# Attention turns with unnormalised probabilities, the reciprocals spread by TensorE onto the outputs, and part c's products made in the input projection

## The chip, the cores and the metric

One core of a Trainium2 chip runs the whole program. The metric is the device time of one execution in microseconds (us), the median of several.

## What is computed

One step of a two-layer streaming encoder over 576 tokens: 512 of a new stream and 64 of a running one. Each layer makes one combined input projection and, from it, three parts: A, sliding-window attention; B, a gated MLP over positions; C, retention. The three are scaled, joined and projected by `w_out`; then a SwiGLU feed-forward follows. Each half ends in a norm and is added to the stream. The change is in A, and in the place of C's last product:

```
s = einsum('...lhgd,...mhd->...hglm', q, k) * HEAD_DIM**-0.5      # own chunk of 64 and two chunks before
p = softmax(concatenate([s, sink], -1))[..., :-1]                 # a learned sink per head joins the sum
a = einsum('...hglm,...mhd->...lhgd', p, v)
...
c = head_group_norm(r, ret_g) * silu(g_c)
merged = concatenate([rms_norm(a), rms_norm(b), c]) @ w_out
```

## The kernel before

Everything is kept transposed, features on partitions and tokens along the free axis. The tokens are cut into two groups, 256 (g = 0) and 320 (g = 1), for the large products. Each of these is made in float32 precision of three passes (L454 to L456): a weight tile is split into a high half (ScalarE, `w_hi`) and a low half (VectorE, `w_lo`, L1230), and so is the moving side (`h_hi`, `h_lo`). The order of each engine's work is written out by hand; semaphores tie the engines. ScalarE's work is recorded at one line, L878, whatever it is.

Attention runs after the input projection, in nine chunks of 64 queries, eight heads in four pairs. It is a pipeline by turns. In turn c

- TensorE makes the scores of chunk c+1 (L707, 64x64 tiles, banks 0/1 or 2/3), the transposes of the probabilities of chunk c-1 (`turn`: L722, the first 128 keys; L724, the other 64), and the values of chunk c-2 (`values`, L744: a wide part of 128 keys, a half part of 64);
- VectorE takes the maxima of chunk c (L1484 to L1488), copies the half transposes of chunk c-2 to `halfT` (L1496), adds the sink to the sum of chunk c-1 and inverts it (L1503, L1504), and multiplies the probabilities by it (`normalise`, L1505). Then come one product of the merged input of `w_out` (`merged`, L1518) and one low half of such a product (`lo_of_merged`, L1524);
- ScalarE makes the exponentials of chunk c with their sums, copies the wide transposes to `wideT`, after every second chunk takes the output of a pair of chunks from PSUM (a copy `aT` and a square `sqa`, by `outs`), and makes the high half of one product (`hi_of_merged`).

The merged input has 8 tiles of 128 rows for each group: k = 0 to 3 are A, 4 and 5 are B, 6 and 7 are C. The table `MERGED` (L151) gives their order. The first 8 (B and C) are made in the turns, the 8 of A after the last turn. Outputs of a pair of chunks go to bank 6 or 7 in turn. The last values come between the first output products (`part_out`, tiles of B and C first). GpSimd adds up the squares of A.

In the list below are the functions that the change touches.

## Time and profile before

| | |
|---|---|
| Median of 3 runs | 1372.68 us (1370.81 to 1374.32) |
| The profiled execution | 1367.82 us, of it 1365.8 us of span |
| Busy: TensorE, VectorE, ScalarE, GpSimd | 97%, 49%, 35%, 13% |
| Instructions in the record | 24010 |
| Granted clock of TensorE over the span | 0.992 |

Busy time counts the share of the span in which an engine had an instruction under way. It says nothing of which engine the others waited for; for that one reads the stretch in question. The span runs from the first to the last recorded instruction, and the time of the execution holds 2.0 us more.

### The profile page before, as it was taken

The page shows a single profiled execution, that of the slowest core. Times are in us where ns is not written, and L with a number is a line of the kernel's source. Part 1 is how long each engine was busy: PE and PEld are TensorE (multiplying, and loading weights), DVE is VectorE, ACT ScalarE, POOL GpSimd, SP SyncE. Part 2 cuts the span into 40 slices and gives each one's busy share as a digit, 9 for nine tenths or more (in the row PEclk, how much of TensorE's full clock was granted, in tenths as well). Part 3 has the DMA queues.
Part 4 walks back from the last instruction along what each step waited for, and adds up shares of the span by engine and source line. Part 5 has one row for each costly group of instructions (what it writes and reads, how often), then busy time and mean ns, then how long its engine had stood idle before and what let it go on. Part 6 is the DMA issues. An engine that isn't in the chain of part 4 may idle for free.

```text
span 1365.8 us, 24010 instructions
## 1 busy us (share of the span) xinstructions
PE 1321.8 (97%) x10374; PEld 1283.9 (94%) x10374; DVE 663.2 (49%) x1158; ACT 482.3 (35%) x994; POOL 182.4 (13%) x223
## 2 busy tenths in 40 slices
PE   8999979999999999999999997899999999999996
PEld 8999859999999999999999996699999999999996
DVE  6556773854444444211467487656544444431113
ACT  5223365642232233222333236655422322332220
POOL 6202123500000000010340021252000000001110
PEclk9999999999999999999999999999999999999998
DMA  4412101222222222222232120021322222222212
GB/s 168 170 63 66 56 1 46 80 99 87 78 84 87 78 84 87 78 92 79 78 109 96 60 74 32 1 93 61 109 79 78 92 79 78 92 79 78 93 47 70
DMA packets 33322, 107.94 MB, mean 79 GB/s; under 512 B 4144, under 2 KB 8640, under 8 KB 33216
## 3 DMA queue, kind: packets, MB, share of 16 engines
q1 hardware_dynamic: 31056, 101.25, 21.7%
q0 software_dynamic: 2160, 5.15, 1.1%
q8 instruction: 82, 1.34, 0.4%
q14 instruction: 24, 0.20, 0.0%
HBM read 103.24 MB, written 3.15 MB: 78 GB/s over the span
## 4 chain that ended last, share of the span: by engine, by line
PE 87%; DVE 8%; issue 2%; ACT 0%; POOL 0%; POOLq 0%; DVEq 0%; ACTq 0%
PE psum L454 27%; PE psum L456 27%; PE psum L455 27%; DVE h_lo L1237 1%; DVE x L1285 1%; PE psum L474 1%; DVE mx L1484 1%; DVE rsq L1372 1%; PE psum L464 1%; PE psum L573 1%; DVE prob L1505 1%; PE psum L570 1%; PE psum L744 0%; DVE y_ffn L1283 0%; DVE y_mix L1283 0%
## 5 line engine op out<-in xcount | busy, mean ns | idle before, releaser
L454 PE MATMUL psum<-h_hi,w_hi 128*128 128x320 f32 (+1 forms) x2192 | 656.1, 299 | 3.5 <-DVE hid_whole L1274 2.5
L455 PE MATMUL psum<-h_lo,w_hi 128*128 128x320 f32 (+1 forms) x2192 | 649.2, 296 | 0.0
L456 PE MATMUL psum<-h_hi,w_lo 128*128 128x320 f32 (+1 forms) x2192 | 649.2, 296 | 0.0
L454 PEld LDWEIGHTS psum<-h_hi,w_hi 128*128 128x128 f32 x2192 | 415.7, 190 | 8.6 <-DVE hid_whole L1274 2.9
L455 PEld LDWEIGHTS psum<-h_lo,w_hi 128*128 128x128 f32 x2192 | 415.9, 190 | 0.3
L456 PEld LDWEIGHTS psum<-h_hi,w_lo 128*128 128x128 f32 x2192 | 415.8, 190 | 0.0
L1230 DVE TENSOR_TENSOR w_lo<-raw,w_hi 128x1024 fp32r<-128x1024 f32 x184 | 230.8, 1262 | 325.9 <-ACT w_hi L878 325.9
L878 ACT ACTIVATE w_hi<-raw 128x1024 fp32r<-128x1024 f32 x184 | 192.3, 1050 | 180.0 <-DMA raw<-in_wts 179.8
L456 PE MATMUL psum<-hid_hi,w_lo 128*128 128x256 f32 (+1 forms) x672 | 199.6, 297 | 0.0
L455 PE MATMUL psum<-hid_lo,w_hi 128*128 128x256 f32 (+1 forms) x672 | 197.7, 294 | 0.0
L454 PE MATMUL psum<-hid_hi,w_hi 128*128 128x256 f32 (+1 forms) x672 | 197.1, 293 | 0.0
L1694 POOL TENSOR_TENSOR acc<-acc,sq 128x320 f32<-128x320 f32 (+1 forms) x105 | 104.6, 996 | 246.8 <-ACT sq L878 238.3
L454 PEld LDWEIGHTS psum<-hid_hi,w_hi 128*128 128x128 f32 x672 | 126.5, 188 | 0.0
L455 PEld LDWEIGHTS psum<-hid_lo,w_hi 128*128 128x128 f32 x672 | 126.3, 188 | 0.0
L456 PEld LDWEIGHTS psum<-hid_hi,w_lo 128*128 128x128 f32 x672 | 126.0, 187 | 0.0
L878 ACT ACTIVATE hid_hi<-hid_whole 128x256 fp32r<-128x256 f32 (+1 forms) x84 | 36.2, 445 | 192.3 <-DVE hid_whole L1583 192.3
L1691 POOL COPY acc<-sq 128x256 f32<-128x256 f32 (+1 forms) x15 | 11.8, 797 | 634.9 <-ACT sq L878 634.9
L1274 DVE TENSOR_TENSOR hid_whole<-psum,rstd 128x256 f32<-128x256 f32 (+1 forms) x84 | 38.1, 453 | 103.0 <-PE psum L456 103.0
L878 ACT ACTIVATE gate_whole<-gate_whole 128x256 f32<-128x256 f32 (+1 forms) x84 | 37.1, 445 | 138.8 <-DVE gate_whole L1274 138.8
L1274 DVE TENSOR_TENSOR gate_whole<-psum,rstd 128x256 f32<-128x256 f32 (+1 forms) x84 | 38.1, 453 | 64.2 <-PE psum L456 48.5
L1250 DVE RECIPROCAL rec<-std 128x2 f32<-128x2 f32 (+1 forms) x36 | 4.3, 151 | 103.7 <-ACT std L878 103.7
L1237 DVE SCALAR_TENSOR_TENSOR h_lo<-x,sp,h_hi 128x256 fp32r<-128x256 f32 (+1 forms) x64 | 50.7, 843 | 3.2 <-ACT h_hi L878 3.1
(178 smaller groups left out, 1054.9 us busy)
## 6 DMA issues: line engine op xcount, KB each, us to landing
raw<-in_wts SPq DMA_DIRECT2D x184, 512.0 KB, 3.2
x<-in_xT SPq DMA_DIRECT2D x2, 640.0 KB, 10.2
tab<-in_tabs POOLq DMA_DIRECT2D x2, 640.0 KB, 4.2
lp<-in_lpar POOLq DMA_DIRECT2D x2, 640.0 KB, 6.8
out_x<-x SPq DMA_DIRECT2D x4, 320.0 KB, 2.3
tab<-in_tabs POOLq DMA_DIRECT2D x2, 577.0 KB, 5.3
x<-in_xT SPq DMA_DIRECT2D x2, 512.0 KB, 5.4
out_x<-x SPq DMA_DIRECT2D x4, 256.0 KB, 2.1
```

The costliest lines, as they stand in the source:

```text
L454: pe.matmul(out, wh, hi, start=first, stop=False)
L455: pe.matmul(out, wh, lo, start=False, stop=False)
L456: return pe.matmul(out, wl, hi, start=False, stop=last)
L464: mm = pe.matmul(banks[bank][0:n, SUM_AT + i:SUM_AT + i + 1], src[:, t0:t0 + n], ones[:, 0:1], start=True, stop=True)
L474: mm = pe.matmul(banks[bank][:, c:c + n], rec[0:n, b:b + 1].to_broadcast([n, P]), ident[0:n, 0:n], start=True, stop=True)
L570: pe.matmul(out, vtok[0:n, b, e], inner[0:n, b % 2, hh, 0:n], start=True, stop=state is None)
L573: pe.matmul(out, state[:, half, e], qxi[:, half, t0:t0 + n], start=False, stop=half == 1)
L878: return act.activation(out, in_, f, **kw)
L1230: dve.tensor_tensor(w_lo[:, r, :], raw[:, r, :], w_hi[:, r, :].bitcast(F32), ALU.subtract)\
L1237: dve.scalar_tensor_tensor(out=h_lo[g][:, k, :], in0=x[:, k, cols(g)], scalar=sp[:, l, c:c + 1], in1=h_hi[g][:, k, :].bitcast(F32), op0=AL ...
L1274: return dve.tensor_tensor(out, bank, rstd[:, cols(g)], ALU.mult)
L1694: pool.tensor_tensor(acc[:, cols(g)], acc[:, cols(g)], buf, ALU.add).then_inc(sq_added, 1)
```

## The change

- VectorE no longer multiplies the probabilities. The transposes wait for the exponentials alone (`p_ready`), and the values are made of unnormalised probabilities.
- The reciprocals (`rd`, now made by `divisors`) lie one to a query, on partitions. TensorE spreads them (`spread_rd`): four matmuls per chunk, with the reciprocal of a head pair broadcast to 64 weight columns and the identity as the moving side, into bank 7. ScalarE copies that bank to `rs` for each pair of chunks (`rs_copy`), VectorE multiplies the outputs from PSUM by it into `aT` (`scale_out`), and ScalarE squares `aT` (`a_square`).
- All outputs go to bank 6.
- The four products of C come first in `MERGED`, and are made in the input projection, in place in `rT`, after its tile 16. Those of B follow in the turns 1 to 4. The output products of group 0 wait for six low halves instead of four.

```diff
-MERGED = [(g, k) for ks in (range(4, KT), range(4)) for g in (0, 1) for k in ks]
+MERGED = [(g, k) for ks in ((6, 7), (4, 5), range(4)) for g in (0, 1) for k in ks]
...
+        def product(g, k):
+
+            return h_whole[g][:, k, :] if k < 6 else rT[:, k - 6, cols(g)]
...
                 def turn(c):
...
-                    pe.wait_ge(pn_ready, L(c + 1, CHUNKS))
+                    pe.wait_ge(p_ready, L(c + 1, CHUNKS))
...
                 def values(c):
...
-                    elif c >= 4 and c % 2 == 0:
-                        pe.wait_ge(a_taken, L(b - 1, NB))
+                    elif c % 2 == 0:
+                        pe.wait_ge(a_scaled, L(b, NB))
...
-                            out = banks[6 + b % 2][64 * h:64 * h + 64, :].rearrange("p (j n) -> p j n", n=P)
+                            out = banks[6][64 * h:64 * h + 64, :].rearrange("p (j n) -> p j n", n=P)
...
+                def spread_rd(c):
+
+                    b, at = c // 2, c % 2 * CHUNK
+                    if c == 0:
+                        pe.wait_ge(ro_taken, L(NB, NB))
+                        pe.wait_ge(state_ready, L(NB, NB))
+                    elif c % 2 == 0:
+                        pe.wait_ge(rs_ready, L(b, NB))
+                    pe.wait_ge(rd_ready, L(c + 1, CHUNKS))
+                    for jj in (0, 1):
+                        for h in (0, 1):
+                            out = banks[7][64 * h:64 * h + 64, :].rearrange("p (j n) -> p j n", n=P)
+                            i = 2 * h + jj
+                            mm = pe.matmul(out[:, 2 * jj:2 * jj + 2, at:at + CHUNK],
+                                           rd[:, c % 2, i:i + 1].to_broadcast([P, CHUNK]),
+                                           ident[:, :].rearrange("p (s q) -> p s q", q=CHUNK), start=True, stop=True,
+                                           tile_position=(0, 64 * h))
+                    mm.then_inc(rd_spread, 1)
...
                     if c == CHUNKS + 1:
-                        part_out(0, bc, 4)
+                        part_out(0, bc, 6)
                     if c >= 2:
                         values(c - 2)
-                part_out(1, bc, 4)
+                    if 1 <= c < CHUNKS + 1:
+                        spread_rd(c - 1)
+                part_out(1, bc, 6)
...
-                def outs(b):
+                def rs_copy(b):
+                    n = TB[b][1]
+                    act.wait_ge(rd_spread, L(min(2 * b + 2, CHUNKS), CHUNKS))
+                    if b:
+                        act.wait_ge(a_scaled, L(b, NB))
+                    fn(rs[:, :, 0:n], grid(b, banks[7], 4), ACT.Copy).then_inc(rs_ready, 1)
+
+                def a_square(b):
                     t0, n = TB[b]
-                    act.wait_ge(o_done, L(min(2 * b + 2, CHUNKS), CHUNKS))
-                    fn(aT[:, :, t0:t0 + n], grid(b, banks[6 + b % 2], 4), ACT.Copy)
+                    act.wait_ge(a_scaled, L(b + 1, NB))
                     if b:
                         act.wait_ge(a_ssq, L(b, NB))
-                    fn(sqa[:, :, 0:n], grid(b, banks[6 + b % 2], 4), ACT.Square).then_inc(a_taken, 1)
+                    fn(sqa[:, :, 0:n], aT[:, :, t0:t0 + n], ACT.Square).then_inc(a_taken, 1)
...
                     if c >= 3 and c % 2:
-                        outs((c - 3) // 2)
+                        rs_copy((c - 3) // 2)
+                    if c >= 5 and c % 2:
+                        a_square((c - 5) // 2)
...
+                more[16].append(lambda: [merged(n) for n in range(4)])
...
-                def normalise(c):
+                def divisors(c):
                     dve.wait_ge(p_ready, L(c + 1, CHUNKS))
-                    o, n = WINDOW[c]
                     if c >= 2:
-                        dve.wait_ge(pn_ready, L(c - 1, CHUNKS))
+                        dve.wait_ge(rd_spread, L(c - 1, CHUNKS))
                     link(dve.tensor_tensor(rd[:, c % 2, :], den[:, c % 2, :], es[:, c % 2, :], ALU.add))
-                    link(dve.reciprocal(rd[:, c % 2, :], rd[:, c % 2, :]))
-                    dve.tensor_tensor(prob[:, c % 2, :, o:o + n], prob[:, c % 2, :, o:o + n],
-                                      rd[:, c % 2, :].unsqueeze(2).to_broadcast([P, 4, n]), ALU.mult)\
-                       .then_inc(pn_ready, 1)
...
+                    dve.reciprocal(rd[:, c % 2, :], rd[:, c % 2, :]).then_inc(rd_ready, 1)
+
+                def scale_out(b):
+                    t0, n = TB[b]
+                    dve.wait_ge(o_done, L(min(2 * b + 2, CHUNKS), CHUNKS))
+                    dve.wait_ge(rs_ready, L(b + 1, NB))
+                    dve.tensor_tensor(aT[:, :, t0:t0 + n], grid(b, banks[6], 4), rs[:, :, 0:n], ALU.mult)\
+                       .then_inc(a_scaled, 1)
...
-                        normalise(c - 1)
-                    if 1 <= c <= EARLY:
-                        if c == 1:
-                            dve.wait_ge(rstd_kept, L(KEPT["b"] + 2, KEPTS))
-                            dve.wait_ge(c_ready, L(4, 4))
-                        merged(c - 1)
+                        divisors(c - 1)
+                    if c >= 4 and c % 2 == 0:
+                        scale_out((c - 4) // 2)
+                    if 1 <= c <= EARLY - 4:
+                        merged(c + 3)
                     if 2 <= c <= EARLY + 1:
                         lo_of_merged(c - 2)
+                scale_out(NB - 1)
```

On TensorE, in the middle of the attention turns, the order before runs from the transposes of one chunk (L722, L724) over the values (L744) and the scores (L707) to the next transposes:

```order
L722 MATMUL psum<-ident,prob 128x128 [waits pn_ready,half_ready,pt_ready]
L724 MATMUL psum<-ident,prob 64x128
...
L744 MATMUL psum<-wideT,vk 64x4x64 [waits half_ready,pt_ready,a_taken]
L744 MATMUL psum<-wideT,vk 64x4x64
L744 MATMUL psum<-halfT,vk 64x4x64 x2
L707 MATMUL psum<-kk,qq 64x192 [waits p_ready]
L707 MATMUL psum<-kk,qq 64x192 x7
```

In the changed kernel the same place (its lines L730, L732 the transposes, L750 the values, L767 the spread of `rd`, L715 the scores) reads, for one turn and the spread of the next:

```order
L730 MATMUL psum<-ident,prob 128x128 [waits p_ready,half_ready,pt_ready]
L732 MATMUL psum<-ident,prob 64x128
...
L750 MATMUL psum<-wideT,vk 64x4x64 [waits half_ready,pt_ready,a_scaled]
L750 MATMUL psum<-wideT,vk 64x4x64
L750 MATMUL psum<-halfT,vk 64x4x64 x2
L767 MATMUL psum<-ident,rd 64x2x64 [waits rd_ready]
L767 MATMUL psum<-ident,rd 64x2x64 x3
L715 MATMUL psum<-kk,qq 64x192 [waits p_ready]
L715 MATMUL psum<-kk,qq 64x192 x7
...
L767 MATMUL psum<-ident,rd 64x2x64 [waits rd_ready,rs_ready]
```

Four matmuls now stand between the half values and the scores, and the transposes name `p_ready` in place of `pn_ready`.

On VectorE, one turn before is this (a turn that has all its parts; `mx`, `nm`, `sm` are the maxima):

```order
L1484 TENSOR_REDUCE mx<-psum 128x4 [waits p_ready,s_done]
L1486 SCALAR_TENSOR_TENSOR nm<-mx,nsink 128x4 [waits dve_chain]
L1488 TENSOR_TENSOR sm<-nm,nsink 128x4 [waits dve_chain]
L1496 COPY halfT<-psum 64x512 [waits o_done,pt_done]
L1503 TENSOR_TENSOR rd<-den,es 128x4 [waits pn_ready,p_ready]
L1504 RECIPROCAL rd<-rd 128x4 [waits dve_chain]
L1505 TENSOR_TENSOR prob<-prob,rd 128x768 [waits dve_chain]
L1518 SCALAR_TENSOR_TENSOR h_whole_100<-ub,sp,gv 128x320
L1524 TENSOR_TENSOR h_lo_52<-h_whole_99,h_hi_50 128x256 [waits hhi_ready]
```

In the changed kernel an even turn of the middle, with the multiply of a pair of chunks (L1563), is this:

```order
L1538 TENSOR_REDUCE mx<-psum 128x4 [waits p_ready,s_done]
L1540 SCALAR_TENSOR_TENSOR nm<-mx,nsink 128x4 [waits dve_chain]
L1542 TENSOR_TENSOR sm<-nm,nsink 128x4 [waits dve_chain]
L1550 COPY halfT<-psum 64x512 [waits o_done,pt_done]
L1556 TENSOR_TENSOR rd<-den,es 128x4 [waits rd_spread,p_ready]
L1557 RECIPROCAL rd<-rd 128x4 [waits dve_chain]
L1563 TENSOR_TENSOR aT<-psum,rs 128x4x128 [waits rs_ready,o_done]
L1569 TENSOR_TENSOR h_lo_52<-h_whole_100,h_hi_50 128x256 [waits hhi_ready]
```

The multiply of the probabilities is gone, the multiply of the outputs stands in every second turn, and from turn 5 on there is no product.

At the end of the input projection VectorE before goes from the reciprocals of B's norm (L1250) to the split of a weight tile (`w_lo`) and the last evictions:

```order
L1250 RECIPROCAL rec<-std 128x2 [waits tok_std] x2
L1250 RECIPROCAL rec<-std 64x1
L1230 TENSOR_TENSOR w_lo<-raw,w_hi 128x1024 [waits hi_made]
L1274 TENSOR_TENSOR qq<-psum,rstd 128x256 [waits tile_done]
L1274 TENSOR_TENSOR qq<-psum,rstd 128x320 [waits tile_done]
```

In the changed kernel the four products of C (L1457) stand there:

```order
L1287 RECIPROCAL rec<-std 128x2 [waits tok_std] x2
L1287 RECIPROCAL rec<-std 64x1
L1457 SCALAR_TENSOR_TENSOR rT<-rT,sp,sg 128x256 [waits c_ready]
L1457 SCALAR_TENSOR_TENSOR rT<-rT,sp,sg 128x256
L1457 SCALAR_TENSOR_TENSOR rT<-rT,sp,sg 128x320 x2
L1267 TENSOR_TENSOR w_lo<-raw,w_hi 128x1024 [waits hi_made]
L1311 TENSOR_TENSOR qq<-psum,rstd 128x256 [waits tile_done]
```

They have moved from the turns 3, 4, 7 and 8 to a place ahead of a weight split.

## Rows read from the trace of the kernel before

Times are in us from the start of the span. The first layer's attention runs from 161.31 to 198.32, the second's from 831.95 to 868.23. Names are given as output<-inputs. A row of a timeline has its start, its length, the engine, the line, the operation, the shapes, how many were merged, and in brackets the idle time before it with what ended it. A row of a window has its length, then busy us (and instructions) of PE, PEld, DVE, ACT and POOL, then PEclk, the share of DMA and GB/s.

**Rows 1.** The page: busy time, share of the span and instructions.

```profile
PE 1321.8 (97%) x10374; PEld 1283.9 (94%) x10374; DVE 663.2 (49%) x1158; ACT 482.3 (35%) x994; POOL 182.4 (13%) x223
```

**Rows 2.** Windows: busy time and granted clock; both attention stretches, one slow piece.

```profile
164.00:172.00 8.00, 7.05 (x62) 4.19 (x63) 7.55 (x21) 6.35 (x32) 0.00 (x0) 0.57 0.01 2
161.31:198.32 37.01, 27.48 (x266) 16.17 (x266) 32.99 (x78) 27.73 (x107) 5.78 (x9) 0.86 0.04 14
831.95:868.23 36.28, 23.28 (x267) 14.14 (x266) 32.92 (x78) 27.73 (x107) 5.95 (x9) 1.00 0.05 15
```

**Rows 3.** Waits: who waited for whom, in total, times, longest.

```profile
PE psum L722 <- DVE prob L1505: 19.2, 14, 1.8
```

**Rows 4.** Chain of waits, second layer, 850 to 859 us, by line.

```profile
by line: issue 40.4%; DVE mx L1484 19.5%; DVE h_whole L1518 12.1%; DVE h_lo L1524 11.9%; DVE prob L1505 11.0%; DVE rd L1504 4.2%; DVE nm L1486 3.9%; DVE rd L1503 3.4%; DVE halfT L1496 1.3%; DVE sm L1488 0.8%
```

**Rows 5.** Timeline of VectorE, one turn of attention in the second layer.

```profile
842.76 0.95 DVE L1484 TENSOR_REDUCE mx<-psum 128x4 f32<-128x768 f32 x1
...
855.50 0.95 DVE L1484 TENSOR_REDUCE mx<-psum 128x4 f32<-128x768 f32 x1
...
856.76 0.68 DVE L1496 COPY halfT<-psum 64x512 f32<-64x512 f32 x1
857.36 0.14 DVE L1503 TENSOR_TENSOR rd<-den,es 128x4 f32<-128x4 f32 x1
...
857.75 0.96 DVE L1505 TENSOR_TENSOR prob<-prob,rd 128x768 f32<-128x768 f32 x1
858.63 0.54 DVE L1518 SCALAR_TENSOR_TENSOR h_whole<-rT,sp,sg 128x320 f32<-128x320 f32 x1
...
859.50 0.95 DVE L1484 TENSOR_REDUCE mx<-psum 128x4 f32<-128x768 f32 x1
```

**Rows 6.** Timeline of TensorE, second layer: start, and one turn.

```profile
835.73 0.60 PE L724 MATMUL psum<-ident,prob 128*64 128x128 f32 x4
836.40 0.88 PE L707 MATMUL psum<-kk,qq 64*64 64x192 f32 x16
...
854.40 0.30 PE L722 MATMUL psum<-ident,prob 128*128 128x128 f32 x1 [1.06 <-DVE prob L1505]
...
855.39 0.65 PE L744 MATMUL psum<-wideT,vk 128*64 128x256 f32 x4
855.97 0.43 PE L744 MATMUL psum<-halfT,vk 64*64 64x256 f32 x2
855.99 0.55 PE L707 MATMUL psum<-kk,qq 64*64 64x192 f32 x4
...
856.46 0.82 PE L707 MATMUL psum<-kk,qq 64*64 64x192 f32 x12
858.86 0.30 PE L722 MATMUL psum<-ident,prob 128*128 128x128 f32 x1 [1.59 <-DVE prob L1505]
```

**Rows 7.** Timeline of TensorE: groups near the added one in shape.

```profile
73.20 0.66 PE L570 MATMUL psum<-inner,vtok 128*64 128x128 f32 x8
73.79 0.45 PE L577 MATMUL psum<-vtok,kz 128*32 128x64 f32 x16
...
159.97 1.42 PE L474 MATMUL psum<-ident,rec 128*128 128x128 f32 x10
```

**Rows 8.** Timeline of ScalarE, second layer.

```profile
852.74 0.60 ACT L878 ACTIVATE aT<-psum 128x512 f32<-128x512 f32 x1 [0.57 <-PE psum L744]
...
855.74 0.62 ACT L878 ACTIVATE wideT<-psum 128x512 f32<-128x512 f32 x1
...
856.87 0.42 ACT L878 ACTIVATE prob<-psum,nm 128x192 f32<-128x192 f32 x1
...
858.47 0.21 ACT L878 ACTIVATE es<-sm 128x4 f32<-128x4 f32 x1
```

**Rows 9.** Timeline of VectorE at the end of the input projection, second layer.

```profile
826.29 1.23 DVE L1230 TENSOR_TENSOR w_lo<-raw,w_hi 128x1024 fp32r<-128x1024 f32 x1 [2.25 <-ACT w_hi L878]
```

More of the change, by code:

```diff
@@ L248, in program @@
         sqa = place("sqa", [P, 4, P])
+        rs = place("rs", [P, 4, P])
         rsq = place("rsq", [P, 2, T])
@@ L354, in program @@
         p_ready = sem("p_ready")
-        pn_ready = sem("pn_ready")
+        rd_ready = sem("rd_ready")
+        rd_spread = sem("rd_spread")
+        rs_ready = sem("rs_ready")
+        a_scaled = sem("a_scaled")
         pt_done = sem("pt_done")
@@ L731, in values @@
                     if c == 0:
-                        pe.wait_ge(ro_taken, L(NB, NB))
-                        pe.wait_ge(state_ready, L(NB, NB))
                         pe.wait_ge(vk_ready, L(2, 2))
-                    elif c >= 4 and c % 2 == 0:
-                        pe.wait_ge(a_taken, L(b - 1, NB))
+                    elif c % 2 == 0:
+                        pe.wait_ge(a_scaled, L(b, NB))
                     pe.wait_ge(pt_ready, L(WIDE[c], WIDE[-1]))
@@ L775, in _ @@
                 pe.wait_ge(p_ready, L(CHUNKS, CHUNKS))
-                part_out(2, bc, 4)
+                part_out(2, bc, 6)
                 spread(l, "a", 0, 4)
-                part_out(3, bc, 4)
+                part_out(3, bc, 6)
                 sum_tokens(l, "a", 1, acc, 5, [(a_ssq, L(NB, NB))])
-                pe.wait_ge(a_taken, L(NB, NB))
+                pe.wait_ge(a_scaled, L(NB, NB))
                 part_out(4, bc, 8)
@@ L1073, in hi_of_merged @@
                     act.wait_ge(prod_ready, L(n + 1, len(MERGED)))
-                    fn(h_hi[g][:, k, :], h_whole[g][:, k, :], ACT.Copy).then_inc(hhi_ready, 1)
+                    fn(h_hi[g][:, k, :], product(g, k), ACT.Copy).then_inc(hhi_ready, 1)
                 for c in range(CHUNKS + 2):
@@ L1085, in _ @@
                     if c >= 3 and c % 2:
-                        outs((c - 3) // 2)
+                        rs_copy((c - 3) // 2)
+                    if c >= 5 and c % 2:
+                        a_square((c - 5) // 2)
                     if 1 <= c <= EARLY:
                         hi_of_merged(c - 1)
-                outs(NB - 1)
+                rs_copy(NB - 1)
+                a_square(NB - 2)
+                a_square(NB - 1)
                 root(l, "a", 0, 4, SWA_HEADS * HD)
@@ L1405, in gate_b, with merged @@
                                       ALU.mult).then_inc(b_ready, 1)
+                def merged(n):
+                    g, k = MERGED[n]
+                    if n == 0:
+                        dve.wait_ge(c_ready, L(4, 4))
+                    if n == 4:
+                        dve.wait_ge(rstd_kept, L(KEPT["b"] + 2, KEPTS))
+                    if k < 4:
+                        src, c, scale = aT[:, k, cols(g)], SP["na"] + k, acc[:, cols(g)]
+                    elif k < 6:
+                        src, c, scale = ub[:, k - 4, cols(g)], SP["nb"] + k - 4, gv[:, 0, cols(g)]
+                    else:
+                        src, c, scale = rT[:, k - 6, cols(g)], SP["rg"] + k - 6, sg[:, k - 6, cols(g)]
+                    dve.scalar_tensor_tensor(out=product(g, k), in0=src, scalar=sp[:, l, c:c + 1],
+                                             in1=scale, op0=ALU.mult, op1=ALU.mult).then_inc(prod_ready, 1)
                 more = {i: [] for i in range(IN_T)}
@@ L1496, in turned @@
                     dve.tensor_copy(halfT[0:CHUNK, c % 2, :], banks[5][0:CHUNK, :]).then_inc(half_ready, 1)
-                def normalise(c):
+                def divisors(c):
                     dve.wait_ge(p_ready, L(c + 1, CHUNKS))
-                    o, n = WINDOW[c]
                     if c >= 2:
-                        dve.wait_ge(pn_ready, L(c - 1, CHUNKS))
+                        dve.wait_ge(rd_spread, L(c - 1, CHUNKS))
                     link(dve.tensor_tensor(rd[:, c % 2, :], den[:, c % 2, :], es[:, c % 2, :], ALU.add))
-                    link(dve.reciprocal(rd[:, c % 2, :], rd[:, c % 2, :]))
-                    dve.tensor_tensor(prob[:, c % 2, :, o:o + n], prob[:, c % 2, :, o:o + n],
-                                      rd[:, c % 2, :].unsqueeze(2).to_broadcast([P, 4, n]), ALU.mult)\
-                       .then_inc(pn_ready, 1)
-                def merged(n):
-                    g, k = MERGED[n]
-                    if k < 4:
-                        src, c, scale = aT[:, k, cols(g)], SP["na"] + k, acc[:, cols(g)]
-                    elif k < 6:
-                        src, c, scale = ub[:, k - 4, cols(g)], SP["nb"] + k - 4, gv[:, 0, cols(g)]
-                    else:
-                        src, c, scale = rT[:, k - 6, cols(g)], SP["rg"] + k - 6, sg[:, k - 6, cols(g)]
-                    dve.scalar_tensor_tensor(out=h_whole[g][:, k, :], in0=src, scalar=sp[:, l, c:c + 1],
-                                             in1=scale, op0=ALU.mult, op1=ALU.mult).then_inc(prod_ready, 1)
+                    dve.reciprocal(rd[:, c % 2, :], rd[:, c % 2, :]).then_inc(rd_ready, 1)
[5 more added lines that the diff above has]
+                       .then_inc(a_scaled, 1)
                 def lo_of_merged(n):
@@ L1523, in lo_of_merged @@
                     dve.wait_ge(hhi_ready, L(HR["merged"] + n + 1, HRS))
-                    dve.tensor_tensor(h_lo[g][:, k, :], h_whole[g][:, k, :],
+                    dve.tensor_tensor(h_lo[g][:, k, :], product(g, k),
                                       h_hi[g][:, k, :].bitcast(F32), ALU.subtract).then_inc(h_ready, 1)
```

## The prediction, made before the changed kernel ran

> **What bounds the kernel now.** The page comes first: TensorE is busy for 97% of the span [rows 1], so most of the time is matmuls that the change leaves alone, and only the stretches where TensorE waits can give anything. The list of waits names the one that matters: the transposes at L722 waited for the normalised probabilities (L1505) 14 times, 19.2 us in all [rows 3]. All of it lies in the attention turns, one stretch in each layer: 37.01 us in the first, 36.28 us in the second, with VectorE busy for 33 us of each, ScalarE 27.7 and TensorE 27.5 or 23.3 [rows 2]. (The records of the first stretch are longer because 8 us of it ran at a granted clock of 0.57, mostly the lower level, 1.2 GHz; the second ran at 1.00.) The chain of waits in a steady piece is made of VectorE's lines alone, "issue" being the time in which its next instruction stands behind the one before [rows 4]. From 842.76 to 859.50 VectorE begins four turns, 4.19 us each, with no wait [rows 5]. TensorE's turn from 854.40 (transposes) to the end of its scores at 856.46 + 0.82 = 857.28 is 2.88 us; then it stands until 858.86 [rows 6]. So VectorE bounds the stretch, at 4.19 a turn against TensorE's 2.88.
>
> **The change on VectorE.** Removed from each turn: the multiply of the probabilities, 0.88 us from its start to the next start [rows 5]; nine per layer, two of them smaller. Four of the eight products leave the turns. Added: one multiply of 512 elements per partition out of PSUM every second turn. The trace has a copy of 512 from PSUM at 0.60 from start to start [rows 5] and I take that, so 0.30 a turn. A turn then is: maxima to copy 1.26, copy 0.60, sum and reciprocal 0.39 [rows 5], 0.30, and a remainder (0.87 before, for product and low half together, about 0.4 for the low half alone): 2.95 us. VectorE stops being the bound.
>
> The four products in the projection stand between the reciprocals and a w_lo split that before waited 2.25 us for ScalarE [rows 9]. Four of about 0.44 (half of 0.87 each [rows 5]) are 1.7 us: they fit, cost nothing, and delay nobody. Were that cover gone, they would delay one split and one PSUM eviction by 1.7 us per layer, behind which TensorE still has a projection tile to do.
>
> **On ScalarE.** An output copy and a square become a copy of the spread reciprocals and a square from SBUF: the same sizes, 0.6 us each as records [rows 8]. Four exps and the small one take 1.81 us (856.87 to 858.68), the wide copy 0.49, a high half some 0.4, the two others 0.5 a turn: 3.2 us a turn. Not the bound.
>
> **On TensorE.** Added: four matmuls of 128x64 weights on 128 columns in each turn, alternating between the two halves of the array's columns. The trace of before has a group of just that form and alternation, the eight records of L570: 0.59 us from its start to that of L577. The serial bound is the spread at L474, 10 records in 161.31 less 159.97, 1.34 us, 1.07 for eight [rows 7]. I take 0.59, since shape and alternation are those of L570. There is a second price. Before, the half-wide values (855.97) and the scores (855.99) start together and end 1.31 us later, though alone they take 0.58 and 0.88 [rows 6]; the new group stands between them, so 0.15 of overlap goes. With one more start of a group I take 0.8 in all: 3.7 us a turn; bounds 0.6 (nothing lost) and 1.3 (serial, and 0.2 lost).
>
> On this a rule bears. The Trainium skill, "TensorEngine Tiling (Array Packing)", Key Properties, says that changing the tiling mode drains the engine, and the added group (128x64) comes between two groups of 64x64. The trace fits it as far as it goes: same tiling, starts 0.02 us apart (855.97, 855.99); from wide to half values 0.58 (855.39, 855.97). By the rule the 0.15 goes; without it the turn would be 3.55 and the gain about 2 us more over both layers.
>
> So TensorE becomes the bound at 3.7 us a turn, against 4.19 now: a gain of 0.5 a turn from the steady part, and more from the last turns, where it has no scores to make and no longer waits for the multiply.
>
> **New waits.** Outputs now use one bank (6) and spread reciprocals one (7), where outputs had both in turn. The even turns' values wait for the scaled outputs of the pair before (VectorE's turn: 1.26 + 0.60 + 0.39 + 0.60, about 2.9 us after it starts its maxima); the transposes and scores ahead of it on TensorE cover that. The odd turns' spread waits for ScalarE's copy, which follows the wide copy, which follows the transposes: 0.04 + 0.49 + 0.60 + 0.06 = 1.19 us after them, while TensorE's values take 1.17 (855.39 to the scores' would-be start, 0.58 twice). Even, so some 0.1 per odd turn. Behind that spread wait the next scores, and VectorE's maxima behind them, which have 0.7 us of slack in a turn.
>
> **The sum, second layer.** Scores of chunk 3 start at 836.40 when the exps of chunk 1 are done [rows 6]; now the first spread stands ahead of them: 837.1. Then scores 0.88, transposes 0.6 (four), half values 0.6, spread 0.7: scores of chunk 4 at 839.9. Scores, eight transposes 1.0, wide values 0.6: 842.4. The first spread into a used bank waits for its copy (maxima of chunk 3 from 838.8, being 1.3 us, exps 1.8, wide copy 0.5, copy 0.6: 843.0): scores of chunk 5 at 843.8. Four turns of 3.7 bring TensorE to the transposes of chunk 7 at 858.6, two turns without scores (1.0 + 1.17 + 0.6) to 864.2. Odd waits add 0.2: the first output product starts at 864.4 instead of 868.23 (the end of the stretch [rows 2]). Gain 3.8 us. From there TensorE is fed in both kernels: the added steps of the tail (multiply, square, three sums of GpSimd) end some 2.3 us after the last values, and the sum over tokens that needs them comes 5 us after; so the gain reaches the end whole.
>
> **First layer.** The same walk at half clock in the piece 164 to 172 [rows 2]: groups that would take 5 us there take more, and now nothing of VectorE's hides it. I take 2.7 us of gain here instead of 3.8 (bounds: 1 if the low clock stays as long as before, 4.5 if a TensorE that waits less is not lowered).
>
> Together 6.5 us. The profiled execution took 1367.8 us (span 1365.8 and 2.0 around it), 4.9 less than the median of the runs, 1372.68; the gain is the same in both: 1372.7 - 6.5 = 1366.2, 0.47% less.
>
> **Rivals.**
> - *The spread costs nothing beside the other work* (0.12 or so): it overlaps its neighbours. For it: L570's records do overlap one another. Against: it lies between groups on other row tilings. The turn is then about 3.3, ScalarE's 3.2 being next: gain some 10 us, 1362.7.
> - *The spread costs its serial price,* 1.3 a turn, or the odd waits grow to that: 4.2 a turn, as now; only the last turns and the late start differ, gain 0 to 3 us: 1371. For it: L474, the other spread by a broadcast weight, shows no overlap.
> - *The other side: the clock.* Now that TensorE bounds the turns, low clock costs in full: a turn takes about 7 us instead of 3.7. Before, 8 us at 0.57 in the first layer cost 0.7 (37.01 against 36.28 [rows 2]), since VectorE hid it. Every 2 us at the lower level cost 1. From 13 us of it beyond what the walk has, over the two layers, the gain is gone; from 21 us the kernel is slower by over 4 us (1377). Against: TensorE will have fewer gaps than now, and the second layer stayed at 1.00 even with gaps of 1.6 us.
> - *It does nothing:* the multiply would have to be off the chain; the 19.2 us of rows 3 speak against it.
>
> **Chances.** The forecast (gain 4 to 9) 0.54, the free spread 0.10, the serial price 0.26, the clock 0.10. The 80% range leaves out the ends of the clock and of the free spread: 1362 to 1372.5; the forecast's own is 1363.5 to 1368.7. A measurement of this kernel tells a change of about 0.3%, 4.1 us, from none: faster takes the forecast, the free spread and a little of the serial case, 0.66; the rest of the serial case and half of the clock's is no change, 0.27; slower 0.07.
>
> **What would show it.** In the profile after: no wait of the transposes for VectorE; starts of the scores 3.6 to 3.8 us apart in mid-stretch; eight records of the spread in about 0.6 us; VectorE idle for some 8 us in each stretch, waiting for scores; the four products ending before the w_lo split; stretches of 32 to 34 us. The prediction is wrong if the spread's group takes over 1 us, if it waits for ScalarE's copy by over 0.5 a turn, or if the granted clock in the second stretch falls under 1.

## The result, and the profile after

| | before | after |
|---|---|---|
| Median of four runs | 1371.74 us (1366.36 to 1374.32) | 1358.22 us (1357.03 to 1359.56) |
| Ratio, 95% interval | | 0.9911 (0.9889 to 0.9933) |
| Profiled execution, and its span | 1367.82 us, 1365.8 | 1357.03 us, 1355.1 |

The change makes the kernel 0.89% faster, 12.2 us by the ratio and 13.5 by the medians; 6.5 us were forecast, and 1358.22 lies below the range (1362 to 1372.5). The kernel before has runs of two lengths, about 1367 and about 1372.5 us, the profiled one being of the shorter, while the four runs of the changed kernel lie within 2.5 us of each other. That is about half of what the prediction missed, and the experiments go after it.

The page of the changed kernel, its busy times:

```profile
PE 1329.3 (98%) x10518; PEld 1288.6 (95%) x10518; DVE 651.1 (48%) x1150; ACT 480.9 (35%) x994; POOL 179.4 (13%) x223
```

Windows of the changed kernel: the attention stretch of each layer, from the first scores to the first output product (columns as in [rows 2]):

```profile
160.99:192.82 31.83, 29.09 (x339) 17.52 (x338) 25.13 (x69) 27.54 (x108) 2.97 (x7) 1.00 0.05 17
825.79:857.61 31.82, 29.08 (x338) 17.52 (x337) 24.78 (x69) 27.54 (x108) 2.97 (x7) 1.00 0.05 16
```

Against [rows 2], the first stretch is 37.01 - 31.83 = 5.18 us shorter and the second 36.28 - 31.82 = 4.46. In both, TensorE is now busy for 29.1 us of 31.8; VectorE has come down from 33 us to 25. The clock, 0.86 in the first stretch before, is 1.00 in both. These 9.6 us are nearly all of the difference of the spans, 10.7. Behind the second stretch both kernels take the same time to the end of the span (1365.8 - 868.23 = 497.6 us, 1355.1 - 857.61 = 497.5).

Waits of the changed kernel over the whole span (who waited for whom: us in total, times, longest). L730 is the first transpose (L722 before), L767 the spread of the reciprocals, L1538 the maxima:

```profile
DVE mx L1538 <- PE psum L715: 7.5, 12, 1.2
...
PE psum L767 <- ACT rs L905: 2.2, 4, 0.8
...
PE psum L730 <- issue: 0.3, 2, 0.2
```

The 19.2 us of [rows 3] are gone: the transposes wait for no other engine. The wait has turned round, VectorE waits for the scores. The chain of waits of the changed kernel between 838 and 852 us, by line, says the same, where [rows 4] had VectorE's lines alone:

```profile
by line: PE psum L750 24.9%; PE psum L715 18.5%; PE psum L730 16.8%; PE psum L767 13.1%; PE psum L732 12.5%; issue 5.5%; ACT rs L905 4.2%; ACT h_hi L905 3.4%; ACT prob L905 2.2%; ACT sqa L905 0.7%; ACT wideT L905 0.2%; ACTq L1101 0.1%; ACTq
```

Timeline of TensorE in the changed kernel, second layer, the start and one full turn:

```profile
829.42 0.63 PE L732 MATMUL psum<-ident,prob 128*64 128x128 f32 x4
829.98 0.66 PE L767 MATMUL psum<-ident,rd 128*64 128x128 f32 x8
830.57 0.88 PE L715 MATMUL psum<-kk,qq 64*64 64x192 f32 x16
...
836.62 0.66 PE L767 MATMUL psum<-ident,rd 128*64 128x128 f32 x8 [0.81 <-ACT rs L905]
837.21 0.88 PE L715 MATMUL psum<-kk,qq 64*64 64x192 f32 x16
...
840.79 0.88 PE L715 MATMUL psum<-kk,qq 64*64 64x192 f32 x16
...
845.27 0.33 PE L730 MATMUL psum<-ident,prob 128*128 128x128 f32 x1
...
846.29 0.65 PE L750 MATMUL psum<-wideT,vk 128*64 128x256 f32 x4
846.87 0.65 PE L750 MATMUL psum<-halfT,vk 64*64 64x256 f32 x4
847.45 0.66 PE L767 MATMUL psum<-ident,rd 128*64 128x128 f32 x8
848.04 0.88 PE L715 MATMUL psum<-kk,qq 64*64 64x192 f32 x16
848.85 0.33 PE L730 MATMUL psum<-ident,prob 128*128 128x128 f32 x1
```

From transposes to transposes is 848.85 - 845.27 = 3.58 us, from 837.21 to 848.04 three turns take 3.61 each. Within a turn: transposes 1.02, wide values 0.58, half values 0.58, spread 0.59, scores 0.81. The eight records of the spread start 0.59 us ahead of the scores, as L570's did ahead of L577 [rows 7].

Timeline of VectorE in the changed kernel: two maxima in mid-stretch, and the end of the input projection, where the four products of C now stand ahead of the w_lo split:

```profile
841.74 0.96 DVE L1538 TENSOR_REDUCE mx<-psum 128x4 f32<-128x768 f32 x1 [0.80 <-PE psum L715]
...
848.99 0.96 DVE L1538 TENSOR_REDUCE mx<-psum 128x4 f32<-128x768 f32 x1 [1.04 <-PE psum L715]
```

```profile
817.81 1.78 DVE L1457 SCALAR_TENSOR_TENSOR rT<-rT,sp,sg 128x256 f32<-128x256 f32 x4
820.14 1.23 DVE L1267 TENSOR_TENSOR w_lo<-raw,w_hi 128x1024 fp32r<-128x1024 f32 x1 [0.54 <-ACT w_hi L905]
```

The products take 1.78 us, and the split still waits 0.54 us for ScalarE where it waited 2.25 [rows 9]: they lie in that gap whole.

### The profile page after: what moved, and what is told of

The parts are those of the page before. It is cut to its first block, busy times and chain, and to the rows that moved or that the text cites. A ratio compares the mean times of both kernels' runs of the same rounds, so it can differ in the third digit from the quotient of the medians.

```text
span 1355.1 us, 24322 instructions
## 1 busy us (share of the span) xinstructions
PE 1329.3 (98%) x10518; PEld 1288.6 (95%) x10518; DVE 651.1 (48%) x1150; ACT 480.9 (35%) x994; POOL 179.4 (13%) x223
## 3 DMA queue, kind: packets, MB, share of 16 engines
q0 software_dynamic: 2160, 5.15, 1.1%
HBM read 103.24 MB, written 3.15 MB: 79 GB/s over the span
## 4 chain that ended last, share of the span: by engine, by line
PE 89%; DVE 5%; ACT 2%; issue 1%; POOL 0%; POOLq 0%; DVEq 0%; ACTq 0%
PE psum L462 27%; PE psum L464 27%; PE psum L463 27%; DVE x L1322 1%; PE psum L482 1%; DVE h_lo L1274 1%; DVE rsq L1409 1%; PE psum L472 1%; PE psum L750 1%; PE psum L581 1%; PE psum L715 1%; ACT prob L905 1%; PE psum L578 1%; PE psum L767 0%; DVE y_ffn L1320 0%
```

## The experiments

Two questions were open. Why are the first layer and the median so much better than forecast (one theory: the low clock is a cost of the kernel before, which its profiled run shows only in part; its rival: the removed work is worth more than was counted, whatever the clock)? And what does each part of the change bring?

**1. TensorE kept busy in the kernel before.** Four dummy matmuls (their result is used by nobody) with the shape of the spread, into the half of bank 5's partitions that the half transposes leave unused, ahead of the transposes of each turn; the results are those of the kernel before.

```diff
+                def fill_gap():
+
+                    for _ in range(4):
+                        pe.matmul(banks[5][64:128, 0:P], ones[:, 0:64], ones[:, :], start=True, stop=True,
+                                  tile_position=(0, 64))
...
                     if 1 <= c < CHUNKS + 1:
+                        fill_gap()
                         turn(c - 1)
```

> The kernel before, with four dummy matmuls (ones against ones, 128x64 weights, 128 columns, about 0.6 us) put into TensorE's gap in every attention turn, ahead of the transposes; the outputs do not change. Theory A (part of the measured gain is the clock: the gaps of TensorE in the attention turns of the kernel before let the granted clock fall, in some runs for long, and the changed kernel has no such gaps): the filled kernel is faster than the kernel before by 1 to 5 us in the medians, its clock reads 0.995 as that of the changed kernel, and its runs lie closer together. Rival B (the clock has no part; the extra gain is in the turns alone): no change, or slower by up to 2 us, and the clock of its runs as before.

Measured: 1369.13 us (1367.50 to 1369.30, 12 runs), ratio 0.9983 (0.9970 to 0.9997). Its windows, both layers:

```profile
162.26:198.64 36.38, 32.28 (x339) 21.76 (x338) 33.01 (x78) 27.77 (x107) 5.95 (x9) 1.00 0.04 15
831.65:868.03 36.38, 32.27 (x338) 21.75 (x337) 33.02 (x78) 27.77 (x107) 5.95 (x9) 1.00 0.04 15
```

VectorE does what it did in [rows 2], the stretches are as long as the second of before, and TensorE's granted clock is 1.00, the higher level, in both. The kernel before ran 29 times beside it: 8 runs at 1366.05 to 1367.68, mean granted clock 0.990 to 0.994, and 21 at 1370.64 to 1373.90, clock 0.983 to 0.989; none between. Of the 12 filled runs none is above 1369.3, all at 0.993 to 0.996. Useless work on TensorE took the longer length away, as the theory of the clock has it. The filled runs lie some 2 us above the shorter group of before, though their stretches are together no longer than in the profile of before (72.8 against 73.3 us). The profile shows 1.0 us of it ahead of the first stretch, which starts at 162.26 instead of 161.31, and 0.7 behind the second. The filler touches neither place. Ahead of the stretch the clock is lower for a while; here is the window of 25 to 35 us, dense products behind a wait of TensorE of 3.15 us, in the kernel before and in the filled one:

```profile
25.00:35.00 10.00, 6.93 (x42) 6.96 (x43) 8.85 (x14) 0.83 (x2) 9.61 (x11) 0.83 0.01 2
25.00:35.00 10.00, 7.20 (x36) 7.22 (x37) 8.67 (x13) 0.58 (x2) 9.61 (x11) 0.66 0.00 0
```

The mean clock there is 0.66 in the profiles of experiments 2 and 3 too, 0.83 in the changed kernel's, and 1.00 in that of experiment 5, which is the kernel before unchanged, so it goes with the run and not with the edit. Profiles thus differ by about a microsecond by low clock far from the attention turns.

**2. The products of C alone.** The kernel before with the new order of `MERGED` and the four products in the projection; the probabilities are still multiplied.

```diff
-MERGED = [(g, k) for ks in (range(4, KT), range(4)) for g in (0, 1) for k in ks]
+MERGED = [(g, k) for ks in ((6, 7), (4, 5), range(4)) for g in (0, 1) for k in ks]
...
+                more[16].append(lambda: [merged(n) for n in range(4)])
...
-                    if 1 <= c <= EARLY:
...
-                        merged(c - 1)
+                    if 1 <= c <= EARLY - 4:
+                        merged(c + 3)
```

> The kernel before with only part c's four products made in the input projection; the probabilities are still normalised. VectorE bounds the turns before, so each product that leaves a turn shortens it by its 0.40 to 0.66 us, about 1.9 us per layer: 3.5 to 4 us faster in all, stretches of about 35.1 and 34.4 us. Rival (VectorE's time in the turns is not all on the chain): under 2 us.

Measured: 1365.54 us (1364.62 to 1368.62, 10 runs, none of the longer length), ratio 0.9968 (0.9952 to 0.9983). Windows: both stretches, and the piece of the second with the low clock.

```profile
162.24:197.53 35.29, 23.27 (x266) 14.18 (x265) 30.68 (x74) 27.66 (x107) 5.35 (x9) 1.00 0.04 15
830.52:867.30 36.78, 25.05 (x266) 14.79 (x266) 30.78 (x74) 27.66 (x107) 5.34 (x9) 0.95 0.04 14
845.00:855.00 10.00, 8.41 (x76) 5.17 (x74) 8.03 (x19) 6.05 (x24) 1.93 (x4) 0.83 0.01 2
```

VectorE's turn shrinks and the stretch at full clock comes down by 1.0 us (36.28 to 35.29), about half of what was expected (1.9 a layer), so not all of VectorE's work in the turns is on the chain; the low piece of the second takes it back. The median is 6.7 us lower than that of the kernel before (4.4 by the ratio), again more than the stretches give, and the longer length is absent. That goes against a simple form of the theory: TensorE has nearly the same gaps here as before, its transposes wait for VectorE 15 times, 20.3 us in all and 1.7 at the longest, against [rows 3]. The shortest runs of this kernel read a mean clock of 0.990, so the mean clock alone doesn't order its runs either. Why ten runs with these gaps have none of the longer length is not known.

**3. The spread alone.** The changed kernel with the products of C back in the turns.

```diff
-MERGED = [(g, k) for ks in ((6, 7), (4, 5), range(4)) for g in (0, 1) for k in ks]
+MERGED = [(g, k) for ks in (range(4, KT), range(4)) for g in (0, 1) for k in ks]
...
-                more[16].append(lambda: [merged(n) for n in range(4)])
...
-                    if 1 <= c <= EARLY - 4:
-                        merged(c + 3)
+                    if 1 <= c <= EARLY:
+                        merged(c - 1)
```

> The changed kernel with part c's products back in the turns. If TensorE bounds the turns at 3.6 us, VectorE's turn of 3.0 to 3.5 us has room for them: within 1 us of the changed kernel, stretches of about 32 us. Rival (VectorE still bounds): 3 to 4 us slower than the changed kernel, stretches near 33.7.

Measured: 1358.42 us (1358.11 to 1360.36, 4 runs), ratio 0.9912 (0.9887 to 0.9938). Windows:

```profile
162.45:194.29 31.84, 29.08 (x338) 17.51 (x337) 27.26 (x73) 27.58 (x108) 3.29 (x7) 1.00 0.05 17
827.31:859.15 31.84, 29.07 (x338) 17.51 (x337) 27.25 (x73) 27.58 (x108) 3.29 (x7) 1.00 0.05 17
```

VectorE has 2.1 to 2.5 us more to do in each stretch than in the changed kernel, and the stretch is as long (31.84 against 31.83 and 31.82). The medians agree too (1358.42 and 1358.22). The spread and the outputs' multiply are the whole gain; the products of C give 1.0 us a layer while VectorE bounds the turn and nothing once TensorE does.

**4. The spread twice.** `for jj in (0, 1, 0, 1)` in `spread_rd`: each matmul is made again, with the same results.

> The changed kernel with each spread of the reciprocals made twice into the same place (eight matmuls in place of four); the outputs do not change. If TensorE bounds the turns and a spread costs its own 0.59 us, each of the 9 spreads but the first three adds 0.59 to 0.65 us: 7 to 9 us slower than the changed kernel in all, turns of 4.2 us, so about 1362 to 1366. Rival (a spread overlaps its neighbours, or another engine bounds): under 3 us.

Measured: 1364.67 us (1363.45 to 1366.05, 10 runs), ratio 0.9951 (0.9936 to 0.9965), 6.4 us above the changed kernel, a little less than the 7 to 9 expected (the "about 1362 to 1366" there doesn't follow from them: 1358.2 and 7 to 9 is 1365 to 1367). Its TensorE timeline, and the windows of both stretches:

```profile
843.16 0.88 PE L715 MATMUL psum<-kk,qq 64*64 64x192 f32 x16
...
846.15 1.09 PE L767 MATMUL psum<-ident,rd 128*64 128x128 f32 x16
847.18 0.88 PE L715 MATMUL psum<-kk,qq 64*64 64x192 f32 x16
```

```profile
161.34:196.40 35.06, 32.97 (x410) 21.44 (x410) 25.41 (x69) 27.77 (x108) 3.38 (x7) 1.00 0.04 15
829.37:865.90 36.53, 34.44 (x410) 22.26 (x409) 25.42 (x69) 27.80 (x108) 3.37 (x7) 0.95 0.04 15
```

Sixteen records stand 1.03 us ahead of the scores where eight stood 0.59 ahead: the second eight cost 0.44, so about 0.15 of the 0.59 belongs to the change of group and not to the columns. The stretch at full clock is 3.2 us longer, against 9 x 0.44 = 4.0 if each turn paid in full; twice 3.2 is the 6.4 of the medians. That TensorE bounds the turns is shown: what is added there lengthens the kernel.

**5, 8, 9, 10. The kernel before, one profile each,** to catch a run of the longer length.

> The kernel before, unchanged, profiled once more, to see where the granted clock falls in a run of its longer kind (its runs lie either at 1366 to 1368 us with a mean clock of 0.990 to 0.994, or at 1371 to 1374 with 0.985 to 0.989). Theory A (the gaps of TensorE in the attention turns bring the low clock): in a run over 1370 us the windows below 1.00 lie in the two attention stretches, over 15 us of them in all, and the stretches are 38 us or longer. Rival (the low clock lies elsewhere, at the start or at the transitions between the halves): the stretches are as in the first profile, 37.0 and 36.3.

> The kernel before once more, for a profile of its longer kind (1371 to 1374 us, mean clock 0.983 to 0.989). The two profiles so far took 1367.8 and 1367.4 and had stretches of 37.0 and 36.3, and 37.0 and 36.8. Theory A (gaps in the attention turns bring the low clock): if the run is over 1370, the stretches hold over 15 us of windows at the low level and together take 4 us or more above 73. Rival: the low clock lies elsewhere, and the stretches stay at 73 to 74 together.

> As e8_before_third: a further profile of the kernel before, with the same two expectations.

> As e8_before_third: a further profile of the kernel before, with the same two expectations.

None did: 1367.38, 1367.58, 1367.12 and 1366.41 us. So the two expectations, which speak of a run over 1370 us, were not put to the test. The profiles show how the low clock wanders. The second stretch of the first of them:

```profile
830.94:867.71 36.77, 24.71 (x266) 14.88 (x265) 33.01 (x78) 27.77 (x107) 5.95 (x9) 0.95 0.04 14
```

Its first stretch was 36.98 us; those of the other three were 37.00, 37.43 and 36.57, their second ones 36.28, 36.27 and 36.27. So in these profiles a stretch of the kernel before takes 36.3 with the clock at 1.00 and up to 37.4 with low pieces. Between the two stretches lie 633.6 us in the first and third profile of this kernel and 633.0 in the other three, so 0.6 us come and go there without any change.

**11, 12. The filler of experiment 1 in one layer only** (`if l == 0:`, then `if l == 1:`, ahead of `fill_gap()`).

> The kernel before with the dummy matmuls of e1 in the gaps of the first layer's attention turns alone. No profile of the kernel before fell into its longer kind (1371 to 1374 us); e1 had none of it in 12 runs. Theory A (gaps of the first layer bring it): all runs under 1370, as e1. Rival B (gaps of the second layer): most runs still at 1371 or longer. If each layer brings a part, the runs lie between, with a spread of 3 us or so.

> The kernel before with the dummy matmuls of e1 in the gaps of the second layer's attention turns alone. Theory A (the first layer brings the longer kind): most runs still at 1371 or longer. Rival B (the second layer does): all under 1370. If each layer brings a part, the runs lie between.

Measured: 1369.57 us (1366.10 to 1372.72) and 1369.39 us (1367.07 to 1372.15), 11 runs each; ratios 0.9996 (0.9979 to 1.0013) and 0.9991 (0.9975 to 1.0007). Both spread over the whole distance that the filler in both layers had closed, so, by the expectations, each layer brings a part. (They ran on another chip than experiment 1, where the kernel before also has three runs at 1368.6 to 1368.9 us, between its two lengths.) The profiled run of the first, 1372.72 us, is as long as the longer runs of before. Its windows: the second stretch, which isn't filled, and pieces of it and of the output products behind it.

```profile
832.04:870.24 38.20, 29.01 (x267) 16.58 (x266) 32.75 (x78) 27.51 (x107) 5.16 (x9) 0.83 0.04 14
```

```profile
840.00:849.00 9.00, 8.47 (x72) 5.01 (x68) 8.40 (x21) 6.66 (x26) 1.43 (x3) 0.63 0.01 3
...
861.00:870.00 9.00, 7.19 (x34) 3.42 (x32) 6.04 (x12) 6.07 (x17) 1.90 (x3) 0.65 0.01 3
870.00:876.00 6.00, 6.00 (x33) 4.43 (x32) 0.00 (x0) 1.74 (x4) 1.73 (x5) 0.66 0.00 0
```

Two low pieces instead of one or none. The stretch is 1.9 us longer than at full clock, VectorE hiding most of it. The second piece runs on into the output products, where TensorE is busy for 6.00 of 6.00 us and nothing hides a low clock: 6 x (1 - 0.66) = 2.0 us. Together 3.9 us in one layer, in a trace whose code in that layer is that of the kernel before. From this stretch to the end of the span are 500.6 us instead of 497.6, so another 1.0 us came later. The first stretch, filled, had a low piece too, at a mean clock of 0.96, and took 37.96 us; so did the filled second stretch of experiment 12's profile, with the same two numbers, while its unfilled first one has 0.86 and 36.90 us. In these few profiles a filled stretch has less low clock than most unfilled ones; the filler doesn't rule it out.

The Trainium skill, "TensorE: Matmul & The Clock Gate", HAM oscillation, says that idle time of the engine is what lets its clock fall. The filled kernels fit that. The page names longer gaps than the 1 to 1.8 us that TensorE has in the turns of the kernel before [rows 3, 6]; here the clock fell behind such gaps (in the second stretch of experiment 11's profile within 1 us of the end of gaps of 1.71 and 1.77 us), so on this point the trace differs from the page. That a gap of this length doesn't always bring it is shown by experiment 2 and by the stretches at 1.00.

**6. The copy of the reciprocals ahead of the exps.** The changed kernel spends 0.81 us in mid-stretch and 0.29 at the end on ScalarE's copy of bank 7. Here ScalarE makes that copy first in its turn.

```diff
                 for c in range(CHUNKS + 2):
+                    if c >= 3 and c % 2:
+                        rs_copy((c - 3) // 2)
                     if c < CHUNKS:
                         exps(c)
...
-                    if c >= 3 and c % 2:
-                        rs_copy((c - 3) // 2)
```

> The changed kernel with ScalarE's copy of the spread reciprocals at the head of the odd turns, ahead of the exponentials, instead of behind the wide copy. Theory (TensorE bounds the turns, and its waits for this copy, 0.81 us at the third spread and 0.29 at the last in each layer, are on the chain): 2 to 2.5 us faster than the changed kernel. Rival (the exponentials come later by the copy and the scores then wait for them): same or slower by 1 to 2 us.

Measured: 1356.60 us (1354.15 to 1357.91, 6 runs), ratio 0.9898 (0.9880 to 0.9916). Windows:

```profile
161.03:191.30 30.27, 28.64 (x339) 17.60 (x338) 24.79 (x69) 27.02 (x108) 2.93 (x6) 1.00 0.05 18
824.33:855.92 31.59, 30.12 (x339) 18.37 (x338) 25.16 (x69) 27.23 (x108) 2.93 (x6) 0.95 0.05 17
```

At full clock the stretch is 1.56 us shorter than in the changed kernel. The medians are 1.6 us apart, where 2 to 2.5 were expected. In the second layer a low piece took 1.3 of it back, now in full view, since TensorE bounds. It stands right behind the wait of the third scores for the exponentials, which every kernel here has:

```profile
827.15 1.07 PE L715 MATMUL psum<-kk,qq 64*64 64x192 f32 x16 [1.33 <-ACT es L905]
```

TensorE does nothing from 826 to 827 us and works without a break from 828 to 831, where the granted clock is 0.50 of full speed, the lower level. The low pieces of experiments 4 (second layer) and 7 (first layer) stand at the same place.

**7. The spread ahead of the values as well.** Experiment 6, and the spread moved between the transposes and the wide values.

```diff
-                    if c >= 2:
-                        values(c - 2)
                     if 1 <= c < CHUNKS + 1:
                         spread_rd(c - 1)
+                    if c >= 2:
+                        values(c - 2)
```

> As e6, and on TensorE the spread stands ahead of the values, so that the half values and the scores, both 64x64 tiles, are neighbours again and the tiling changes less often. By the price that the prediction gave the lost overlap, 0.15 us a turn in six turns of two layers: 1.8 us faster than e6. Rival (no overlap was lost, or VectorE's reciprocals come too late for the earlier place): same as e6, or slower by the wait.

Measured: 1352.37 us (1351.19 to 1353.34, 5 runs), ratio 0.9866 (0.9846 to 0.9887). The window of its second stretch, and TensorE in one turn:

```profile
824.21:853.17 28.96, 27.13 (x339) 18.06 (x338) 24.49 (x68) 27.13 (x108) 3.04 (x6) 1.00 0.05 18
```

```profile
842.04 0.33 PE L730 MATMUL psum<-ident,prob 128*128 128x128 f32 x1
...
843.06 0.66 PE L767 MATMUL psum<-ident,rd 128*64 128x128 f32 x8
843.55 0.60 PE L750 MATMUL psum<-wideT,vk 128*64 128x256 f32 x4
844.08 0.43 PE L750 MATMUL psum<-halfT,vk 64*64 64x256 f32 x2
844.10 0.55 PE L715 MATMUL psum<-kk,qq 64*64 64x192 f32 x4
...
845.31 0.33 PE L730 MATMUL psum<-ident,prob 128*128 128x128 f32 x1
```

The turn is 3.27 us instead of 3.58. The spread stands 0.49 us ahead of its neighbour of the same shape (0.59 ahead of the scores), the half values and the scores start 0.02 us apart again, as in [rows 6]. The stretch at full clock is 1.31 us shorter than in experiment 6 (28.96 against 30.27), more than the 0.9 a layer that was expected; the medians are 4.2 us apart, expected 1.8. (The first stretch had a low piece, clock 0.94, and took 30.04 us.) This is the best version: 5.9 us faster than the changed kernel by the medians, 18 faster than before.

## Why the prediction was right and wrong

The measured median lies 14.5 us under the 1372.7 that the prediction started from, and 6.5 were forecast. By the two profiles the 8.0 us that are missing lie so: 0.7 in the second layer's stretch, 2.5 in the first's, 1.1 outside the stretches, and 3.7 between profile and median (14.5 less the 10.8 by which the two profiled executions differ). The steps that failed are the two that priced the low clock: "2.7 us of gain here instead of 3.8" in the first layer, which measured 5.18, and "the gain is the same in both", which measured 10.8 in the profiled executions and 13.5 in the medians.

**What bounds, and what goes.** Right. The transposes no longer wait, TensorE bounds the turns (the chain; experiment 4), VectorE waits for the scores, by 7.5 us over both layers. Its idle time in a stretch, 31.8 less 25, is 6.7 to 7 us, forecast 8; half of it is this wait.

**TensorE's turn.** Right: 3.61 us, forecast 3.7. L570 was the right row for the spread, 0.59 forecast and measured. The lost overlap exists: by experiment 7 (against experiment 6, whose turn is 3.58 like the changed kernel's) the place of the spread costs 3.58 - 3.27 = 0.31 a turn, of it 0.10 in the spread itself and 0.21 in the values and scores, where 0.15 was counted. By the Trainium skill, "TensorEngine Tiling (Array Packing)", Key Properties, the change of tiling drains the engine; experiments 4 and 7 fit that, with 0.15 and 0.10 us for the spread's side of it.

**The waits.** The first spread into a used bank waited 0.81 us for its copy, where the walk has 0.6 (842.4 to 843.0); the next odd turn loses 0.09 (840.79 to 848.04 is 7.25 us, two turns of 3.58 are 7.16), 0.1 forecast. The wait of 0.29 us at the last spread was not forecast.

**The products of C.** Free in the projection, as forecast (2.25 to 0.54 us of idle time). That they bring nothing was in the sum without being said: with TensorE as the bound no term contained them. Experiment 3 shows it.

**Second layer.** 4.46 us against 3.8. The walk ended 0.6 us late: it let the first spread push the scores of chunk 3 to 5.15 us after the stretch's start, where they start at 4.78 (830.57 less 825.79), and took the four turns at 3.7 instead of 3.61. A term mis-sized, by 0.6 of 32.

**First layer.** 5.18 us against 2.7, above its upper bound of 4.5. The term "2.7 us of gain here instead of 3.8" priced the low clock as something that stays and that TensorE would now pay in full. It didn't stay: in the profiled run the window has 1.00 (the variants of experiments 4, 6 and 7 show that it can fall in this kernel too, and then costs 1.1 to 1.5 us a stretch). 0.73 us of the 5.18 is low clock that before had cost (37.01 against 36.28). The remainder of the profiled difference, some 1.1 us, lies outside the stretches: 0.3 ahead of the first, 0.7 between the two, 0.1 behind. The 0.7 is the 0.6 us that come and go in the unchanged kernel too, so most of this is luck of the pair of profiles and no work of the change.

**The median.** Here the larger step failed: "the gain is the same in both", the profiled execution being 4.9 us under the median. Why it was under wasn't asked. The profiled run belongs to the shorter group; two thirds of the runs before (21 of 29, and 6 of 11 and 13 of 21 in later sets) read a lower mean clock and take about 5.5 us longer. All four runs of the changed kernel are within 2.5 us, and the runs of its variants in experiments 3, 4, 6 and 7 within 2.2 to 3.8. From the shorter group's 1367 to 1358.2 the gain is 8.8 us (the two profiled executions, 10.8 apart, lie at the far ends of their groups); that the longer group has disappeared brings the other 3.4 of the 12.2. The rival on the clock looked at the right quantity, with its sign reversed for this kernel: it asked what low clock would cost after, and not what it costs before. The prediction's own remark that TensorE "will have fewer gaps than now" was the argument, used only to doubt a loss.

**Open.** No run of the kernel before of the longer length was caught with a profile; that its extra time lies in the low pieces and in the products behind them rests on the mean clocks of the runs and on experiment 11, whose second layer has that code. All five profiles of the kernel before are of the shorter length, though two thirds of its timed runs are of the longer. That the closed gaps are what removed the longer length from the changed kernel rests on experiment 1, and experiment 2, which has the gaps and not the longer length, speaks against it as the whole cause. Low clock outside the attention, as at 25 to 35 us, is a rival for a part that no run here separates. What decides in which run the clock falls, and how often, isn't known. Nor can fewer gaps be the whole rule, since experiments 4, 6 and 7 had a low piece in one stretch each.

## What to carry to other kernels

Before a saving is subtracted from a median, look at whether the profiled run is one of the median's kind: the spread of the runs tells, and their mean clock in part. Where TensorE waits a microsecond or more in every turn, the price of these gaps may be a lower clock afterwards, in products where nothing covers it; an edit that closes them may be worth more than the waits it removes. Once the bound moves, edits that lighten the old one bring nothing (experiment 3), and the order of groups on the new one does: here it helped to keep groups of the same tiling next to each other (experiment 7), and to make the copy that frees a bank first in its engine's turn (experiment 6).

## What was unexpected of the hardware

In one set of 29 runs an unchanged program on one core has two run lengths, 1366.1 to 1367.7 and 1370.6 to 1373.9 us, with mean granted clocks of 0.990 to 0.994 and 0.983 to 0.989; in later sets on another chip a few runs lie between. Four dummy matmuls a turn, about 1 us of TensorE (32.27 less 23.28 over nine turns), removed the longer one in 12 runs. In experiments 4, 6, 7 and 11 the granted clock fell to the lower level right behind single waits of TensorE of 1.3 to 1.8 us, but not behind each of them. The same eight matmul records take 0.49 us ahead of a group of their own tiling and 0.59 ahead of one of another, and eight more of them 0.44.
